# A second buffer set for the experts' second-layer weights, and weight rows of twice the length

## The reference, cut to what matters

```python
D_MODEL = 1024; SEQ = 256; N_EXPERTS = 32; TOP_K = 4; D_EXPERT = D_MODEL

def moe_ffn(h, router_w, router_b, w1, b1, w2, b2):
    logits = (xt @ router_w + router_b).astype(jnp.float32)
    top_v, top_e = lax.top_k(logits, TOP_K)
    gate = jax.nn.softmax(top_v, axis=-1)
    ...
    def expert_block(args):
        rows, e = args
        xb = xt[rows]
        hb = xb @ w1[e] + b1[e]
        g, u = hb[:, :D_EXPERT], hb[:, D_EXPERT:]
        g = jnp.minimum(g, SWIGLU_LIMIT)
        u = jnp.clip(u, -SWIGLU_LIMIT, SWIGLU_LIMIT)
        glu = g * jax.nn.sigmoid(g * SWIGLU_ALPHA)
        return ((u + 1.0) * glu) @ w2[e] + b2[e]
    ...
    out = jnp.zeros((N, D), y.dtype).at[row_tok].add(y * row_w[:, None].astype(y.dtype))
```

## Time and profile before

| | |
|---|---|
| median of 3 runs | 2233.08 us (2230.53 to 2280.92) |
| profiled execution | 2232.53 us |
| its span, first to last instruction | 2230.7 us |
| mean granted clock of PE | 0.974 of full speed |
| busy: PE, DVE, ACT | 2091.8, 701.3, 448.3 us |
| moved from HBM | 587.48 MB, 265 GB/s over the span |

### The profile page before, as it was taken

How to read it: one execution, slowest core, us unless ns; L and a number is a source line. 1 busy time by engine, 2 the same in 40 slices (tenths; PEclk the granted TensorE clock), 3 DMA queues, 4 the chain that set the end, 5 groups by cost and what they waited for, 6 DMA issues and landing times.

```text
span 2230.7 us, 29842 instructions
## 1 busy us (share of the span) xinstructions
PE 2091.8 (94%) x10964; PEld 1191.7 (53%) x10965; DVE 701.3 (31%) x1479; ACT 448.3 (20%) x874; POOL 0.2 (0%) x4
## 2 busy tenths in 40 slices
PE   6999989899989999999999999899999999999997
PEld 3767757433333333322222333366489986748996
DVE  2223223311111111111111111213357753525776
ACT  1322230100000000000000000112245431114443
POOL 0000000000000000000000000000000000000000
PEclk8999989899989999999999999999999999999999
DMA  9244663489988999999999989963166545432652
GB/s 352 91 161 179 227 191 137 201 360 417 417 313 329 417 417 417 417 416 417 417 416 417 417 333 418 389 155 124 32 176 191 176 135 132 151 104 86 196 170 84
DMA packets 225886, 590.97 MB, mean 265 GB/s; under 512 B 14667, under 2 KB 114562, under 8 KB 189860
## 3 DMA queue, kind: packets, MB, share of 16 engines
q1 hardware_dynamic: 223804, 587.69, 71.1%
q10 hardware_dynamic: 2024, 2.46, 0.4%
HBM read 587.48 MB, written 2.62 MB: 265 GB/s over the span
## 4 chain that ended last, share of the span: by engine, by line
PE 76%; DMA 9%; SPq 7%; DVE 3%; issue 2%; ACT 2%; ACTq 0%; DVEq 0%
PE psum L1746 13%; PE psum L1931 11%; DMA lower<-in_exp_w 8%; PE psum L1397 7%; PE psum L1770 7%; PE psum L1943 5%; PE psum L1499 5%; SPq L814 5%; PE psum L1504 5%; PE psum L1531 2%; PE psum L1790 2%; PE psum L1714 2%; SPq L811 2%; PE psum L1478 2%; PE psum L1484 1%
## 5 line engine op out<-in xcount | busy, mean ns | idle before, releaser
L1746 PE MATMUL psum<-lower,upper 128*64 128x512 f32 x2176 | 492.7, 602 | 28.8 <-DMA lower<-in_exp_w 28.8
L1746 PEld LDWEIGHTS psum<-lower,upper 128*64 128x64 f32 x2176 | 147.7, 137 | 373.1 <-issue 288.4
L1931 PEld LDWEIGHTS psum<-rounded 128*128 128x128 f32 x2112 | 258.6, 189 | 3.4
L1931 PE MATMUL psum<-rounded 128*128 128x256 f32 x2112 | 260.1, 283 | 0.0
L1770 PE MATMUL psum<-upper 128*64 128x512 f32 x1088 | 240.5, 595 | 8.0 <-ACT upper L1166 8.0
L2392 DVE TENSOR_SCALAR upper<-psum 128x512 f32<-128x512 f32 x34 | 23.5, 692 | 700.3 <-PE psum L1746 698.6
L1397 PE MATMUL psum<-upper,lower 128*128 128x256 f32 (+1 forms) x880 | 167.7, 392 | 4.1 <-ACT upper L961 4.1
L1770 PEld LDWEIGHTS psum<-upper 128*64 128x64 f32 x1088 | 75.3, 137 | 152.6 <-issue 137.0
L1397 PEld LDWEIGHTS psum<-upper,lower 128*128 128x128 f32 (+1 forms) x880 | 130.2, 175 | 37.1 <-issue 12.4
L1943 PE MATMUL psum<-rounded 128*128 128x512 f32 x528 | 128.8, 392 | 2.4 <-DVE rounded L2588 2.4
L1161 ACT ACTIVATE upper<-upper 128x512 f32<-128x512 f32 x32 | 20.2, 630 | 506.1 <-DVE upper L2392 506.1
(11 more groups left out here) (374 smaller groups left out, 1777.4 us busy)
## 6 DMA issues: line engine op xcount, KB each, us to landing
lower<-in_exp_w SPq DMA_DIRECT2D x256, 1024.0 KB, 17.0
upper<-in_exp_w SPq DMA_DIRECT2D x256, 512.0 KB, 17.5
lower<-in_ffn_w_up SPq DMA_DIRECT2D x88, 512.0 KB, 5.3
lower<-in_mod_w SPq DMA_DIRECT2D x12, 2048.0 KB, 10.3
lower<-in_w_in SPq DMA_DIRECT2D x12, 2048.0 KB, 9.1
lower<-in_ffn_w_down SPq DMA_DIRECT2D x44, 512.0 KB, 5.7
lower<-in_odd_w_in SPq DMA_DIRECT2D x8, 2048.0 KB, 11.6
lower<-in_even_w_in SPq DMA_DIRECT2D x7, 2048.0 KB, 11.7
```

The source lines that it names most:

```text
L1746: ins = pe.matmul(bank[first_bank + r // 2][64 * half:64 * half + 64], rows, w1[k][:, 512 * r:512 * r + 512], start=False, stop=(k == W1_O ...
L1931: ins = pe.matmul(bank[4 + b][:, T * g:T * g + T], w[:, g, k, :], x[:, k, :], start=(k == m == 0), stop=(k == KD - 1 and m == 2))
```

## The change

Three things are changed together.

*Longer rows.* Two chunks of 128 rows are loaded by one DMA of 2 MB (`w1`) or 1 MB (`w2`). Partition p gets rows 2p and 2p + 1 of the pair, which lie one behind the other in HBM: 16 KB in one piece in place of 8 KB, and 8 KB in place of 4 KB. The rows of the weights are thereby dealt to the partitions in another order, and what they are multiplied with must follow: the transposes and the extra gather read every second column (`of_chunk`). A pair has one semaphore, and its buffer is refilled when both of its chunks are used.

*A second set for `w2`.* The weights of odd experts go to a second set of buffers of 32 KB a partition behind the first. SP loads `w2` two experts ahead, `w1` one. The set's place overlaps the place of `cb`, so `cb` is fetched after the last use of `w2`. And it overlaps places of the first block; before the first load of the second set SP waits for the last job, and there it also stores the bias rows and waits for the end of that store.

*Loops over pairs.* So that each half of the code names its set, the loops of PE and SP run over pairs of experts, with the body of one expert written out twice.

On DVE the addition of the table (L2490 before) moves behind two copies.

```diff
-        w2 = [arena.view(at_e + 1024 * k, 1024) for k in range(KD)]
+        w1_pair = [arena.view(phase + 4096 * j, 4096) for j in range(KD // 2)]
+        def of_chunk(v, k):
+            at = 2 * P * (k // 2)
+            return v[:, at:at + 2 * P].rearrange("q (p s) -> q s p", s=2)[:, k % 2, :]
...
+        at_w2 = (at_e, arena.at)
+        w2 = [[arena.view(at_w2[c] + 1024 * k, 1024) for k in range(KD)] for c in range(2)]
+        w2_pair = [[arena.view(at_w2[c] + 2048 * j, 2048) for j in range(KD // 2)] for c in range(2)]
...
-                    sp.dma_start(cb, a["const_b"]).then_inc(consts_b_in, 16)
...
-            def load_expert(e, wait_chunk, wait_output):
+            def expert_rows(name, e, j):
                 which = slice(e, e + 1) if isinstance(e, int) else bass.ds(e, 1)
+                return a[name][0, which, 2 * P * j:2 * P * j + 2 * P, :].rearrange("o (p s) n -> (o p) (s n)", s=2)
+            def load_first(e, wait_pair):
                 for n, k in enumerate(W1_ORDER):
-                    wait_chunk(n)
+                    if n % 2:
+                        continue
+                    wait_pair(n + 1)
                     if n == 0:
                         sp.dma_start(exp_b1[0:P:32, :], a["exp_b1"][0, which, :].rearrange("o (r n) -> (o r) n", r=4))\
                           .then_inc(b1_in, 16)
-                    sp.dma_start(w1[k], expert_row("exp_w1", e, slice(P * k, P * k + P))).then_inc(w1_in[k], 16)
-                for k in range(KD):
-                    wait_output(k)
-                    sp.dma_start(w2[k], expert_row("exp_w2", e, slice(P * k, P * k + P))).then_inc(w2_in[k], 16)
+                    sp.dma_start(w1_pair[k // 2], expert_rows("exp_w1", e, k // 2)).then_inc(w1_in[k], 16)
+            def load_second(e, c, wait_pair):
+                for j in range(KD // 2):
+                    wait_pair(2 * j + 1)
+                    sp.dma_start(w2_pair[c][j], expert_rows("exp_w2", e, j)).then_inc(w2_in[c][2 * j], 16)
...
+            def bias_rows_left(k):
+                if k == 1:
+                    empty(sp, n_jobs - 1)
+                    sp.wait_ge(bias_row_ready, 1)
+                    sp.dma_start(scratch, bias_row[0:8, :].rearrange("p (o n) -> p o n", o=1).to_broadcast([8, P, 384]))\
+                      .then_inc(bias_stored, 16)
+                    sp.wait_ge(bias_stored, 16)
...
-            with sp.Fori(1, N_EXP) as e:
-                load_expert(e, lambda n: wait_used(w1_used, e * KD + (n + 1 - KD)),
-                            lambda k: wait_used(w2_used, e * KD + (k + 1 - KD)))
+            load_first(0, panels_left)
+            load_second(0, 0, gates_left)
+            load_second(1, 1, bias_rows_left)
+            with sp.Fori(0, N_EXP // 2 - 1) as pair:
+                for c in range(2):
+                    load_first(pair * 2 + (1 + c), lambda n: wait_used(w1_used, pair * (2 * KD) + (KD * c + n + 1)))
+                    load_second(pair * 2 + (2 + c), c, lambda k: wait_used(w2_used, pair * (2 * KD) + (KD * c + k + 1)))
+            load_first(N_EXP - 1, lambda n: sp.wait_ge(w1_used, (N_EXP - 2) * KD + n + 1))
...
-            sp.wait_ge(bias_row_ready, 1)
-            sp.dma_start(scratch, bias_row[0:8, :].rearrange("p (o n) -> p o n", o=1).to_broadcast([8, P, 384]))\
-              .then_inc(bias_stored, 16)
-            sp.wait_ge(bias_stored, 16)
+            sp.wait_ge(w2_used, N_EXP * KD)
+            sp.dma_start(cb, a["const_b"]).then_inc(consts_b_in, 16)
+            sp.dma_start(gate_b[0:1], a["odd_gate_b_2"]).then_inc(consts_b_in, 16)
...
-                    ins = pe.transpose(bank[7][:, P * j:P * j + P], xg[:, P * j:P * j + P], ident)
+                    ins = pe.transpose(bank[7][:, P * j:P * j + P], of_chunk(xg, j), ident)
...
-                    pe.wait_ge(w1_in[k], 16 * e + 16)
+                    pe.wait_ge(w1_in[k - k % 2], 16 * e + 16)
...
-                    pe.wait_ge(w2_in[k], 16 * e + 16)
-                    ins = output_chunk(bank[6], hiddenT, k)
+                    pe.wait_ge(w2_in[c][k - k % 2], 16 * pair + 16)
+                    ins = output_chunk(bank[6], hiddenT, k, c)
...
-            with pe.Fori(0, N_EXP) as e:
-                expert(e)
+            with pe.Fori(0, N_EXP // 2) as pair:
+                for c in range(2):
+                    expert(pair * 2 + c, pair, c)
```

More of the change, by code:

```diff
@@ L656, in program @@
         places_done, gatesT_ready, route_ready = sem("places_done"), sem("gatesT_ready"), sem("route_ready")
-        w1_in = [sem(f"w1_chunk{k}_in") for k in range(KD)]
-        w2_in = [sem(f"w2_chunk{k}_in") for k in range(KD)]
+        w1_in = {k: sem(f"w1_rows{P * k}_in") for k in range(0, KD, 2)}
+        w2_in = [{k: sem(f"w2_set{c}_rows{P * k}_in") for k in range(0, KD, 2)} for c in range(2)]
         b1_in = sem("expert_b1_in")
@@ L1763, in turn_hidden, with output_chunk, output_sums @@
                 for j in range(4):
-                    ins = pe.transpose(o[:, P * j:P * j + P], hidden[:, P * j:P * j + P], ident)
+                    ins = pe.transpose(o[:, P * j:P * j + P], of_chunk(hidden, j), ident)
                 ins.then_inc(done, 1)
-            def output_chunk(o, rows, k):
+            def output_chunk(o, rows, k, c):
                 for half in range(2):
                     ins = pe.matmul(o[64 * half:64 * half + 64], rows[:, k % 4, 64 * (k // 4):64 * (k // 4) + 64],
-                                    w2[k][:, 512 * half:512 * half + 512], start=(k == 0), stop=(k == KD - 1),
+                                    w2[c][k][:, 512 * half:512 * half + 512], start=(k == 0), stop=(k == KD - 1),
                                     tile_position=(0, 64 * half))
                 return ins
-            def output_sums(ready, n, e, used=None):
+            def output_sums(ready, n, pair, c, used=None):
                 pe.wait_ge(ready, n)
                 for k in range(KD):
-                    pe.wait_ge(w2_in[k], 16 * e + 16)
-                    ins = output_chunk(bank[6], hiddenT, k)
+                    pe.wait_ge(w2_in[c][k - k % 2], 16 * pair + 16)
+                    ins = output_chunk(bank[6], hiddenT, k, c)
                     if used:
@@ L1813, in gather_more @@
                     for i in range(NT):
-                        pe.matmul(bank[7][:, SLOTS * k:SLOTS * k + SLOTS], h2[:, i, P * k:P * k + P],
+                        pe.matmul(bank[7][:, SLOTS * k:SLOTS * k + SLOTS], of_chunk(h2[:, i, :], k),
                                   select_ov[:, i, :], start=(i == 0), stop=(i == NT - 1))
@@ L1826, in next_rows, with further_pass @@
                 pe.wait_ge(xg_copied, e + 2)
-            def further_pass(n, e):
+            def further_pass(n, e, pair, c):
                 gather_more(n, bank[5])
@@ L1837, in further_pass, with two_passes @@
                 for k in range(KD):
-                    pe.wait_ge(w2_in[k], 16 * e + 16)
-                    ins = output_chunk(bank[4], hiddenT_ov, k)
+                    pe.wait_ge(w2_in[c][k - k % 2], 16 * pair + 16)
+                    ins = output_chunk(bank[4], hiddenT_ov, k, c)
                 ins.then_inc(ov["y"], 1)
                 spread_out(ov["y_copied"], n, spreadT_ov, y_ov, ov["done"])
-            def two_passes(n, e):
+            def two_passes(n, e, pair, c):
                 gather_more(n, bank[5])
@@ L1875, in one_pass, with expert @@
                 turn_gathered(e + 2)
-                output_sums(hiddenT_ready, e + 1, e, w2_used)
-            def expert(e):
+                output_sums(hiddenT_ready, e + 1, pair, c, w2_used)
+            def expert(e, pair, c):
                 count = pe.value_load(counts_int_i[0:1, bass.ds(e, 1)], min_val=0, max_val=T)
@@ L1886, in expert @@
                     with pe.If(count > 2 * SLOTS):
-                        further_pass(before + 1, e)
+                        further_pass(before + 1, e, pair, c)
                         with pe.If(count > 3 * SLOTS):
-                            further_pass(before + 2, e)
-                    two_passes(after, e)
+                            further_pass(before + 2, e, pair, c)
+                    two_passes(after, e, pair, c)
                 with pe.Else():
-                    one_pass(e)
-            with pe.Fori(0, N_EXP) as e:
-                expert(e)
+                    one_pass(e, pair, c)
+            with pe.Fori(0, N_EXP // 2) as pair:
+                for c in range(2):
+                    expert(pair * 2 + c, pair, c)
             pe.wait_ge(spread_ready, N_EXP + 1)
@@ L2486, in _ @@
                 empty_job(n)
+            for n in range(n_jobs + 4, first_even):
+                empty_job(n)
             dve.wait_ge(bias_in_b, 32)
@@ L2491, in _ @@
                                       .to_broadcast([P, 8, 384]), ALU.add))
-            for n in range(n_jobs + 4, first_even):
-                empty_job(n)
             for s in range(n_units, len(units) + 2):
```

16 lines of the change are left out of this document (6 added, 10 removed).

## The result

The changed kernel takes 2280.9 us (median of 4 executions, 2278.9 to 2290.0) against 2233.8 for the kernel before on the same chip: a ratio of 1.023, 95% interval 1.021 to 1.025. It is **slower**, by 47 us. One of the kernel before's four executions took 2280.9 us, a slow one, and is left out of the ratio. I had forecast 2256 and no change; the time lies inside my range, the verdict does not. The range is no merit: it held 2280.9 only because it spanned everything from rival 1 (2228) to rival 2 (2319), and neither the forecast (with rival 5 it was 2245 to 2275) nor any rival gives this time.

What follows compares the result with a forecast made beforehand. The prediction took the experts' loop to be bound by PE alone in places and by first-layer weights from 842 to 1257 us. 2232.5 + 2.6 (start, long stretch) + 13.4 + 7.6 (PE's code) = 2256.1 us; range 2228 to 2322.

Steps and rivals of the forecast that it cites:

- rival 1: PE's loop: no more code stalls than before; 2235, or 2228 if longer rows give 1.0 us an expert; chance 0.10.
- rival 2: PE's loop: one branch target displaced in every pair, 7.6 us a pair, sum +86.7, 2319; chance 0.14.
- rival 5: Weight DMAs: longer rows give nothing, 2271; chance 0.61 together with the forecast.
- PE's code: Experts' loop on PE: first entry into expert 27's copy +13.4 us, displaced copy at expert 7 +7.6 us.
- the middle: Displaced copy at expert 7: +7.6 us taken between 0 (all kept) and 15.2 (experts 7 and 28 enter anew).
- The start: Loop's start: bias rows' store and w2(1) go ahead of w1(1), so expert 5 ends 11.3 us later.
- The long stretch: Weights for experts 8 to 26: 19 x 0.64 us gained, so expert 27 begins only 2.6 us later than before.
- the longer rows: Weight DMAs: 29.6 us an expert for 30.2, gain 0.64 us where weights bound, none where PE bounds.
- A second set: Second-layer weights in the experts' loop: never waited for, so a second buffer gains nothing in steady state.
- The rest: Strided transposes 0 (bounds 0 to 4.5 us); fewer DMAs and waits, work after the loop, bias addition: 0.
- rival 4: Whole kernel: faster by over 2%, needs 44 us; weights never binding would save 40.7; chance 0.02.
- Rival 3: PE's loop: every far jump misses, three a pair, adding 228 us, 2547; chance 0.13.

Runs made afterwards that it cites:

- e27: Not a run: expert 27, counted from 0, the second of the two experts with over 64 rows, which take the two-pass branch.
- e2: Kernel before with only PE's loop written over pairs of experts, two copies of the body: 2272.0 us, ratio 1.015 to 1.020.
- e1: As run: kernel before with the longer rows alone, single loop: 2228.2 us, ratio 0.997 to 0.999. As place in the loop: expert 1.
- e9: Here expert 9, a place in the loop. The run so named: kernel before with experts' row counts cut at 64 (all one-pass), 2191.3 us.
- e26: Not a run: expert 26, counted from 0, the last before the second two-pass expert.
- e29: Not a run: expert 29, counted from 0, a place in the experts' loop.
- e7: Here expert 7, a place in the loop. The run so named: changed kernel, no third and fourth pass code, store behind the loop, 2234.5 us.
- e8: Here expert 8, a place in the loop. The run so named: longer rows alone, PE's two branches in the other order, 2241.0 us.
- e28: Not a run: expert 28, counted from 0, the next after the second two-pass expert.
- e11: Kernel before with experts' row counts cut at 64 (all one-pass) and PE's loop over groups of four experts: 2381.6 us.
- e5: As run: kernel before with longer rows and PE's loop over pairs, no second set: 2268.7 us, ratio 1.013 to 1.020. As place: expert 5.
- e4: Changed kernel with the bias rows' store and SP's wait for it moved behind the experts' loop: 2272.9 us, ratio 1.015 to 1.020.
- e6: As run: kernel before with five more never-run further passes, single loop: 2231.7 us, ratio 0.998 to 1.001. As place: expert 6, first two-pass expert.
- e0: Not a run: expert 0, the first expert of the loop.
- e31: Not a run: expert 31, counted from 0, the last expert of the loop.
- e10: Kernel before with experts' row counts cut at 64 (all one-pass) and PE's loop over pairs: 2193.5 us.
- e3: Changed kernel without the code for a third and fourth pass, which no expert takes: 2246.3 us, ratio 1.002 to 1.008.

## Why the prediction was wrong

**The step that failed is the one on PE's code,** and in it the size, not the mechanism. I counted 13.4 us for e27's first entry and 7.6 for one displaced copy, 21.0 in all, "the middle" between nothing and two. e2, where this step stands alone, has 3.2 us at e1, 12.0 from there to e9, and 22.9 from the end of e26 to e29 (12.5 to 35.4): 38.1, of which 2.7 are given back where the weights bind. Three sizes were off:

- I took one displaced entry at e7; there were three: e7 at 6.7 us, e8 at 6.2, e28 at 12.5. The upper end of my bounds, 15.2, held two.
- For e28 I had seen the case (e27's fetches displace the other copy) and given it nothing. It is the dearest one, 9.4 us of gap, where the first jumps in the trace of before had 4.0 and 4.7. The price that I took from the earlier trace rows was that of one missing target; if at e28 the loop's head and the branch are both missing, two fetches stand one behind the other. That would fit the size, and three packets begin within this gap of the changed kernel (four in e2) against none to two within the shorter ones; but e11's gaps at the loop's head are as long with two packets in them, and no run separates the two targets.
- The first entry of e27's copy cost 22.9 - 12.5 = 10.4 us: 13.4 was on the safe side.

What one entry costs, a gap and some 2.4 to 3.5 us of slow matmuls behind it, was read rightly from the earlier trace rows.

**The start** was right in kind, 15.0 us for 11.3. The store ended at 459.4 (forecast 457), w2(1) went first, and the weights were on the chain before e6. Of the 15.0, e2 has 3.2 at e5's end without any store: e1's entry, which I had called hidden by the wait for w1. It isn't, as the wait then moves on by as much. e4's e6 begins its stall at 620.6, so 6.8 are the store's. Counted from where PE comes to the loop, e1's entry is 5.0 and the store 7.1, of which 1.9 are e0's longer gap. Some 3 of the 15.0 are left beside them. e4 has these 3 as well, most of them at its dearer entry of e1; what makes it dearer than e2's and e5's is open.

**The long stretch and the longer rows** were right: 29.7 us an expert for 29.6, -10.0 for -8.7, and the stretch starts from e7's matmuls, so the stalls ahead of it are carried through it. The delay at the stretch's end, 20.9 where 2.6 + 7.6 = 10.2 was forecast, is off only because it began from 30.9 and not 18.9. Rival 5 is out.

**A second set** was right: no wait for the second layer before or after, and e5 against e4 shows nothing of it from e9 to e27. Since it is worth nothing, the loop over pairs, which it brings with it, has nothing to be paid from.

**The rest.** The transposes over every second column take 208 ns to load in place of 141, and 283 in place of 273 to multiply, between my two bounds; an expert on PE alone takes 1429.77 - 1402.36 = 27.41 us in place of 27.25. I took 0; it is 0.6 us over e28 to e31. The last 4.7 us lie behind the loop. 2.6 of them are at one place, from 1634 to 1647 us, where the second block's first matmuls run at a granted clock of 0.74 (L1554 takes 8.02 us for 6.89); e1, which has nothing changed there, has 2.8 us behind the loop as well, and the same 8.01 for 6.89. So this is a slow clock that can come with either loop; why it falls there is open.

**The rivals.** Rival 1 fell with the gaps at e7, e8, e27 and e28, rival 4 with the time. Rival 2, one target displaced in every pair, did not happen: no packet from 745 to 1290. Displacement happened only behind the two-pass experts, three times. Rival 3, every far jump misses, did not happen either, but e11 shows a kernel in which the entry of every copy does: four copies. By the Trainium skill (Runtime: NRT & Kernel Launch, "Instruction fetch mechanics") there is no cache beyond a sequential window of two pages. e10 speaks against it: from 510 to 1400 us it has three far jumps a pair and no fetch. The same section's other figure, that PE's store holds 128 KiB, eight blocks of 16 KiB, is at least of the right order: what e10's pairs run through, 6 packets from 436 us on, stays, and e11's 15 packets a turn don't. No run here measures it closer, nor which block is dropped.

I had put 0.71 on no change because the cases with one displaced entry or none seemed to hold most of the chance. The evidence for more was in the trace: six packets for one two-pass branch, in a store that had to hold two one-pass copies beside it. I named that sentence under rival 2 and didn't carry it into the sum.

**How the 47 us add up,** in medians against the kernel before of each group: longer rows -4.1 (e1); pairs with them 37.0 (e5), so 41.1 for the pairs, where e2 has 39.7; the second set, the constants at the loop's end and the rest of the reordering 3.6 (e4 less e5, not settled); the store's place 6.5 (changed less e4, 47.1 less 40.6). Sum: -4.1 + 41.1 + 3.6 + 6.5 = 47.1. Each part is the step from one kernel to the next, so that they add up proves nothing; what tests them is e2, which has the pairs without the longer rows.

## What to carry to other kernels

Unrolling a hardware loop by two is not free on an engine whose loop body holds a rare branch: the copies fit as long as only the common path is run, and each turn through the rare one pushes out copies of the common one, which then come back at 6 to 12 us apiece, on the critical path and with a slow clock behind them. Count the packets on the instruction queue of the profile inside the loop before and ask what a second copy adds to the code that is *run through*. Code that is jumped over was free in the single loop (e6), but not beside a second copy (e3), so there it is worth taking out. And a buffer for data that nobody waits for pays for nothing that comes with it: take the part that does pay (here the longer rows) alone.

## What the runs showed of the hardware that I had not expected

- A loop can hold 784 rows of matmuls on PE and cost nothing (e6: 384 and five further passes of 80), and a loop that runs 288 of them a turn in four separate pieces (72 each) can stop at every piece in every turn (e11, 15 packets a turn). The step between is sharp: two copies 2 us, four copies 190.
- The gap at an entry is not one number: 2.2 to 5.6 us at most places, 8.5 to 9.7 at e28 and at each turn of e11.
- Taking out code that is never run made the changed kernel 35 us faster (e3), while adding such code to the single loop changed nothing (e6). Both edits touch hardly anything but code that PE jumps over. So where the pieces lie to each other seems to count when the store is nearly full; no run tests it, and by which rule, these runs don't tell.
- Reading a transpose's input at every second column makes its weight load 67 ns longer (208 for 141 ns).
